# Splitting each chunk of the feed-forward weights in one operation of 2048 columns per engine, in place of two of 1024

## What is computed

```python
def conv_gated_ffn(x, w_up, conv_w, conv_b, w_down):
    gu = x @ w_up                                   # 2048 -> 2 * 5632
    gate, up = gu[..., :D_FF], gu[..., D_FF:]
    gate = causal_depthwise_conv(gate, conv_w, conv_b)   # 3 taps
    return (jax.nn.silu(gate) * up) @ w_down        # 5632 -> 2048

h = h + conv_gated_ffn(rms_norm(h, norm_ffn_g[i]), w_up[i], conv_w[i], conv_b[i], w_down[i])
gate = jax.nn.sigmoid(rms_norm(h, norm_ple_g[i]) @ w_ple_gate[i])
h = h + (p[i] @ w_ple[i]) * gate
```

## Time and profile before

| | |
|---|---|
| median of three runs | 2197.57 us |
| profiled execution, its own time | 2197.45 us |
| its span, first to last instruction | 2195.7 us |
| TensorE matmul busy | 2182.3 us (99%), 11639 instructions |
| TensorE weight load busy | 1888.7 us (86%) |
| VectorE busy | 1471.4 us (67%), 1851 instructions |
| ScalarE busy | 1050.8 us (48%), 1338 instructions |
| GpSimd busy | 56.1 us (3%) |
| mean granted TensorE clock | 0.999 of full speed |
| DMA | 185 GB/s; a chunk of 1 MB lands 4.9 us after its issue |

### The profile page before, as it was taken

One profiled execution on the slowest core, in us unless ns is written; L12 is line 12 of the kernel. 1 busy time (PEld: TensorE's weight loads), 2 busy tenths in 40 slices (PEclk: granted clock), 3 DMA queues, 4 the chain that ended last, 5 costly groups with the idle time before them and its releaser, 6 DMA issues.

```text
span 2195.7 us, 32095 instructions
## 1 busy us (share of the span) xinstructions
PE 2182.3 (99%) x11639; PEld 1888.7 (86%) x11639; DVE 1471.4 (67%) x1851; ACT 1050.8 (48%) x1338; POOL 56.1 (3%) x143
## 2 busy tenths in 40 slices
PE   9999999999999999999999999999999999999998
PEld 8898888888888888888898988888888888888886
DVE  6577577666677766676556765777666677766754
ACT  6555444444444444445554554444444444444554
POOL 5000000000000000000000000000000000000001
PEclk9999999999999999999999999999999999999999
DMA  7644555555555555555556445555555555555553
GB/s 256 205 148 154 192 191 182 196 183 191 191 192 190 191 191 191 191 172 193 188 174 184 134 173 189 181 198 184 192 189 191 191 191 191 191 191 190 174 192 115
DMA packets 233131, 406.44 MB, mean 185 GB/s; under 512 B 14796, under 2 KB 49724, under 8 KB 232936
## 3 DMA queue, kind: packets, MB, share of 16 engines
q1 hardware_dynamic: 231824, 402.15, 55.6%
q0 software_dynamic: 512, 1.76, 0.2%
q10 hardware_dynamic: 728, 1.63, 0.2%
HBM read 403.42 MB, written 2.10 MB: 185 GB/s over the span
## 4 chain that ended last, share of the span: by engine, by line
PE 99%; issue 0%; DVE 0%; ACT 0%; POOL 0%; DVEq 0%; POOLq 0%; ACTq 0%
PE acc L1953 15%; PE tps L1953 15%; PE acc L1589 14%; PE acc L1591 14%; PE acc L1590 14%; PE tps L1962 8%; PE acc L1962 8%; PE tps L1590 4%; PE tps L1591 4%; PE tps L1589 4%; PE tps L1646 1%; PE tps L1582 0%; PE tps L1855 0%; DVE w_lo L1080 0%; PE tps L1835 0%
## 5 line engine op out<-in xcount | busy, mean ns | idle before, releaser
L1080 DVE TENSOR_TENSOR w_lo<-raw,w_hi 128x1024 fp32r<-128x1024 f32 (+1 forms) x768 | 920.7, 1214 | 412.9 <-ACT w_hi L908 271.2
L908 ACT ACTIVATE w_hi<-raw 128x1024 fp32r<-128x1024 f32 x508 | 534.9, 1059 | 618.7 <-PE tps L1591 126.1
L1953 PE MATMUL acc<-xa,w_hi 128*128 128x512 f32 x1408 | 341.0, 391 | 0.0
L1953 PE MATMUL tps<-xa,w_hi 128*128 128x512 f32 x1408 | 339.4, 391 | 0.0
L653 ACT ACTIVATE w_hi<-raw 128x1024 fp32r<-128x1024 f32 (+1 forms) x260 | 262.1, 1042 | 147.5 <-PE acc L1591 143.1
L1953 PEld LDWEIGHTS tps<-xa,w_hi 128*128 128x128 f32 x1408 | 258.7, 188 | 50.1
L1953 PEld LDWEIGHTS acc<-xa,w_hi 128*128 128x128 f32 x1408 | 258.3, 188 | 50.1 <-DVE h L1345 0.4
L1589 PE MATMUL acc<-w_hi,xb_hi 128*128 128x512 f32 x560 | 220.7, 394 | 0.0
L1591 PE MATMUL acc<-w_lo,xb_hi 128*128 128x512 f32 x560 | 218.2, 390 | 0.0
L1590 PE MATMUL acc<-w_hi,xb_lo 128*128 128x512 f32 x560 | 217.8, 389 | 0.0
L1962 PEld LDWEIGHTS acc<-xa,w_lo 128*128 128x128 f32 x1408 | 180.7, 191 | 7.1
(11 more groups left out here) (223 smaller groups left out, 2494.5 us busy)
## 6 DMA issues: line engine op xcount, KB each, us to landing
raw<-in_w_up SPq DMA_DIRECT2D x176, 1024.0 KB, 4.9
raw<-in_w_down SPq DMA_DIRECT2D x88, 1024.0 KB, 4.9
raw<-in_w_out SPq DMA_DIRECT2D x32, 1024.0 KB, 5.0
raw<-in_w_ple_gate SPq DMA_DIRECT2D x32, 1024.0 KB, 5.0
raw<-in_w_in SPq DMA_DIRECT2D x22, 1024.0 KB, 5.2
raw<-in_w_ukv SPq DMA_DIRECT2D x8, 1024.0 KB, 5.3
raw<-in_w_in SPq DMA_DIRECT2D x8, 864.0 KB, 4.9
raw<-in_w_uq SPq DMA_DIRECT2D x6, 1024.0 KB, 5.5
```

Source lines behind the costliest of these rows:

```text
L908: copy(w_hi[:, half_of(m), :], raw[:, c % RAW_SLOTS, (m % 2) * HALF:(m % 2 + 1) * HALF], ACT.Copy).then_inc(hi_done, 1)
L1080: dve.tensor_tensor(w_lo[:, half_of(m), 0:n], raw[:, c % RAW_SLOTS, at:at + n], w_hi[:, half_of(m), 0:n].bitcast(F32), ALU.subtract).then_ ...
L1953: ins = pe.matmul(dst, hi[:, k * BLK + n * P:k * BLK + (n + 1) * P], x_both[:, kt, :, :].rearrange("p a s -> p (a s)"), start=kt == 0, sto ...
```

## The change

In the units a chunk is split by one ScalarE and one VectorE operation over its 2048 columns. They fill two neighbouring slots of `w_hi` and of `w_lo`. Both wait until the second of the two slots is free (`m + 2` in place of `m + 1`), and count their semaphore up by two when all of the chunk is done. `go(a, b)` takes steps of two, so all its bounds are made even, and some of the other steps come one half earlier or later relative to the splits. Outside the units the splits stay as they are.

```diff
@@ ScalarE, split_u @@
-                    act.wait_ge(w_used, l * (2 * CHUNKS) + v * UNIT_HALVES + (m + 1))
-                    copy(w_hi[:, half_of(m), :], raw[:, c % RAW_SLOTS, (m % 2) * HALF:(m % 2 + 1) * HALF],
-                         ACT.Copy).then_inc(hi_done, 1)
+                    act.wait_ge(w_used, l * (2 * CHUNKS) + v * UNIT_HALVES + (m + 2))
+                    both = slice(half_of(m), half_of(m) + 2)
+                    copy(w_hi[:, both, :].rearrange("p a n -> p (a n)"), raw[:, c % RAW_SLOTS, :],
+                         ACT.Copy).then_inc(hi_done, 2)
@@ ScalarE, unit @@
-                        for m in range(a, b):
+                        for m in range(a, b, 2):
                             split_u(l, v, m0 + m + AHEAD)
...
-                    go(2, 9)
+                    go(2, 10)
                     for k in range(2):
                         block_ready(act, l, b0 + k, v)
                         copy(gate_f[:, 2 * k:2 * k + 2, :], acc[k][:, :, S:2 * S], ACT.Copy).then_inc(gate_lo, 1)
-                    go(9, 13)
+                    go(10, 14)
                     act.wait_ge(conv_done, UNITS * l + u + 1)
                     copy(gate_f[:, :, :], conv[:, :, :], ACT.Tanh, scale=0.5).then_inc(tanh_done, 1)
-                    go(13, 17 if with_down else 16)
+                    go(14, 18 if with_down else 16)
                     halves_used(act, l, m0 + 15, v)
                     act.wait_ge(g_done, UNITS * l + u)
                     copy(up_f[:, :, :], tps[:, :, S:2 * S], ACT.Copy).then_inc(up_lo, 1)
                     if with_down:
-                        go(17, 24)
+                        go(18, 24)
@@ VectorE @@
+            def split_both(l, m, v):
+
+                base = l * (2 * CHUNKS) + v * UNIT_HALVES
+                dve.wait_ge(hi_done, base + (m + 2))
+                dve.wait_ge(w_used, base + (m + 2))
+                both = slice(half_of(m), half_of(m) + 2)
+                dve.tensor_tensor(w_lo[:, both, :].rearrange("p a n -> p (a n)"), raw[:, m // 2 % RAW_SLOTS, :],
+                                  w_hi[:, both, :].rearrange("p a n -> p (a n)").bitcast(F32),
+                                  ALU.subtract).then_inc(lo_done, 2)
...
                         go(4, 8)
                         rows_kept()
-                        go(8, 9)
+                        go(8, 10)
...
                     if with_down:
-                        go(16, 17)
+                        go(16, 18)
                         gated()
-                        go(17, 19)
+                        go(18, 20)
                         add_down(0)
-                        go(19, 21)
+                        go(20, 22)
                         add_down(1)
-                        go(21, 23)
+                        go(22, 24)
                         add_down(2)
-                        go(23, 24)
                         add_down(3)
```

More of the change, by code:

```diff
@@ L1377, in go @@
                     def go(a, b):
-                        for m in range(a, b):
-                            split(l, m0 + m + AHEAD, vv)
+                        for m in range(a, b, 2):
+                            split_both(l, m0 + m + AHEAD, vv)
                     def tap(t, ft):
@@ L1418, in unit @@
                         dve.sem_inc(acc_free[k], 2)
-                    go(9, 10)
                     dve.tensor_tensor(gate_f[:, :, :], *by_row(gate_f[:, :, :]), ALU.mult).then_inc(gate_step, 1)
-                    go(10, 11)
+                    go(10, 12)
                     dve.wait_ge(gate_step, 3 * UNITS * l + 3 * u + 3)
@@ L1426, in unit @@
                                           ALU.add).then_inc(conv_step, 1)
-                    go(11, 12)
                     for ft in range(4):
@@ L1431, in unit @@
                                                  ALU.mult, ALU.add).then_inc(conv_step, 1)
-                    go(12, 13)
+                    go(12, 14)
                     for ft in range(4):
@@ L1437, in unit @@
                     ins.then_inc(conv_done, 1)
-                    go(13, 15)
+                    go(14, 16)
                     dve.wait_ge(tanh_done, UNITS * l + u + 1)
@@ L1442, in unit @@
                                              ALU.mult).then_inc(silu_done, 1)
-                    go(15, 16)
                     dve.wait_ge(silu_done, 2 * UNITS * l + 2 * u + 1)
```

## The result

The changed kernel took 2200.84 us, the median of 20 runs (2200.28 to 2201.73), against 2197.5 us for the kernel before in the same session (20 runs, 2196.76 to 2198.16). The ratio is 1.0016, 95% interval 1.001 to 1.0022: 3.3 us more, real and small. The forecast was 2200.3, in the range 2197.9 to 2202.0. By the prediction's measure of 0.2% this is no change, with a cost that can be seen all the same.

The account below looks back on a forecast made before the run. TensorE was taken to bound the kernel. 0 for busy time saved, 0 inside the units and 2.84 us at the two layer ends, on 2197.45 us, gave 2200.3 us, range 2197.9 to 2202.0.

Parts of the forecast that it names:

- TensorE sets the time, and the saved busy time is worth 0: Whole kernel: nearly all of the span is TensorE work, so less work on ScalarE and VectorE gains 0.
- The saving, 39 us on VectorE and 50 on ScalarE: Feed-forward units of both layers: 254 fewer instructions on each engine, 50 and 39 us less busy time.
- 2.29 and 1.92 us for 2048 columns: Merged splits: length expected on VectorE and ScalarE, from slopes of 1.04 and 0.83 ns a column.
- The units cost 0: Inside the units: all added lateness of the pairs is covered before TensorE needs the data, costed at 0.
- The room of 5.2 us: End of a unit's up part: VectorE's sum of up_f ends near 561.1, TensorE needs its banks at 566.3.
- 1.1 us left at the row of rstd: First unit of a layer: copy out of a bank done at 288.6, needed at 289.75; thinnest room inside units.
- At the layer's end L598 becomes late by ScalarE's 0.86 us and by VectorE's hold: Last down block: GpSimd's L598 starts later, waits for VectorE's pair, ends at 976.01; TensorE loses 1.42 us a layer.
- Size: Whole kernel: 2.84 us more, all from the two layer ends, giving 2200.3 us, 0.13% more.
- Rival A: Layer ends: GpSimd not held by a VectorE instruction begun before it; 0.5 to 0.9 us in all, 2198.2 us; chance 0.12.
- Rival B: Layer ends: GpSimd gets in only when VectorE falls idle; 10 us in all, 2207.5 us; chance 0.06, milder form included.
- Rival C: Inside units: rooms smaller than thought through queueing, each microsecond overrun costing 20 us; 2210 to 2230 us; chance 0.07.
- D: Whole kernel: faster, only if the matmul rate rises with fewer instructions elsewhere; no size given; chance 0.03.

Follow-up runs that it names:

- the second experiment: Changed kernel with the last chunk of each unit split in two halves again, other chunks still pairs: 2197.78 us against 2197.47, ratio 1.0001.

## Why the prediction was right

- *TensorE sets the time, and the saved busy time is worth 0.* Shown: VectorE and ScalarE are busy 22 and 49 us less, and three kernels with most or all of the changed order, or all its pairs, are within 0.43 us of the kernel before.
- *The saving, 39 us on VectorE and 50 on ScalarE.* ScalarE's came, of VectorE's only 22. The durations do differ by 39 (508 x 1.222 against 254 x 2.292), but rows of consecutive VectorE instructions overlap by 0.08 us (971.41 + 2.29 = 973.70, the next at 973.62), and the kernel before had 254 more instructions whose ends could overlap so. That this is the difference was not counted out. It costs nothing.
- *2.29 and 1.92 us for 2048 columns.* 2.292 and 1.915. That "three sizes lie on" the slopes is more than the earlier trace rows show, which have two for each engine; VectorE's third, 864 columns, took 1085 ns on the mean, 30 above its line.
- *The units cost 0.* Shown by the 234 pairs of the second experiment. The room of 5.2 us was right in kind (it is the banks' release that comes due first, not the w_lo) and 0.5 too large, for the reason given above: TensorE's need was read from ScalarE's start.
- *1.1 us left at the row of rstd.* The copy ended at 288.49 (288.6 worked out); TensorE did not wait. Its need was read from a ScalarE start here too: 289.75, where TensorE's first matmul on the banks stood at 289.55 before and at 289.39 in the changed kernel, so 0.9 us are left at most. The limit itself was not tried.

```profile
289.55 1.75 PE L1953 MATMUL tps<-xa,w_hi 128*128 128x512 f32 x7
```

- *At the layer's end L598 becomes late by ScalarE's 0.86 us and by VectorE's hold.* Shown: this one pair brings the whole cost, each half of it brings a part, and moving the copy takes it away. GpSimd's end was worked out at 976.01 and TensorE at 976.06, against 975.94 and 975.99 in an execution that ran 0.15 us ahead; 1.42 us a layer became 1.51, 2.84 became 3.0.
- *Size.* Measured 3.3 by the medians (interval 2.2 to 4.8 us) and 3.0 by the spans, against 2.84. The remaining 0.3 us stands outside the spans: the sum took the kernel before's 1.75 us around the span, and this kernel has 2.05. It does not come with the pairs. Of the experiments' kernels, that with one pair only, that with the order only and the two with extra VectorE operations have 1.7 to 1.8, the others 2.0 to 2.2; the cause is open.
- *Rival A (no hold)* is out: L598 took 3.58 us. *Rival B (the hold passes on)* is out: GpSimd came between two VectorE operations. *Rival C (rooms overrun)* is out, and the room is measured. *D (faster)* is out.
- Where I was wrong is outside the sum: the reason given for the hold, a second input in SBUF, is one of at least two.

## What to carry to other kernels

Merging instructions on engines for which the saturated engine never waits saved nothing here, and what stands behind a merged instruction came later by the difference in length. The place to look at was not the loop, where the room was the same every time, but its end, where a different consumer stands behind the last instruction. So a GpSimd step on the path is better placed where VectorE has nothing long in SBUF, or so early that its hold does not matter: here one copy, moved two pairs ahead, undid the whole cost.

## What the runs showed of the hardware that I had not expected

- The hold between GpSimd and VectorE works in both directions: a VectorE operation of 1.22 us took 3.22 when GpSimd's had started 0.26 us before it. With a lead of 0.01 us it was GpSimd that was held (3.41 us in place of 2.39).
- A VectorE operation with one SBUF input over 2048 float32 columns took 1.29 us, little more than half of the two-input one's 2.29, and still held GpSimd.
- After a TensorE wait of 4.73 us the clock fell to its lower level and cost 1.7 us (mean granted clock 0.66 over 5 us); waits of 2.12 us did so in 4 of 20 cases, the two of 1.24 us did not.
